# Cache pages laid four tokens to a partition: one page on 32 partitions

## The reference, cut to what matters

```python
z = x @ w_in                                   # q | k | v | B | C | h
page_sum = sum over tokens of cache_k[page]    # per page and head
gate  = q . (page_sum of the block's 2 pages) / 256
sel   = top 3 of the 8 past blocks by gate     # per sample and head
s     = q . k / 8 - slope[head] * (t - pos)    # over the tokens of the chosen blocks
out   = softmax(s) @ v
x1 = LayerNorm(alpha * x + concat(attn, conv) @ w_out)
y  = LayerNorm(alpha * x1 + (silu(a) * g) @ w_ffn_down)    # a, g = conv3(x1 @ w_ffn_up)
```

## Time and profile before

| | |
|---|---|
| median of 3 runs | 487.06 us |
| the profiled execution's own time | 488.61 us |
| its span in the profile | 486.8 us (1.8 us lie around it) |
| TensorE busy | 432.3 us, 89% |
| VectorE busy | 294.7 us, 61% |
| ScalarE busy | 184.4 us, 38% |
| read from device memory | 121.9 MB |
| SyncE's DMA queue | 107.55 MB |
| ScalarE's DMA queue | 16.78 MB |

### The profile page before, as it was taken

One profiled execution on the slowest core, in us unless ns is written; L12 is line 12 of the kernel. 1 busy time (PEld: TensorE's weight loads), 2 busy tenths in 40 slices (PEclk: granted clock), 3 DMA queues, 4 the chain that ended last, 5 costly groups with the idle time before them and its releaser, 6 DMA issues. The chain is left out here.

```text
span 486.8 us, 8294 instructions
## 1 busy us (share of the span) xinstructions
PE 432.3 (89%) x2951; PEld 352.1 (72%) x2951; DVE 294.7 (61%) x367; ACT 184.4 (38%) x713; POOL 84.1 (17%) x115
## 2 busy tenths in 40 slices
PE   5999969989899993799968797999999996999990
PEld 5678847866767761467524375999999996999990
DVE  0567769999989878526122245257777767243527
ACT  1566446764455433412001122245555553333300
POOL 1003000795120000000000240352122115000002
PEclk9999989999999998799979999899999998999996
DMA  8999998996959999999999963066666684576302
GB/s 306 339 326 386 396 387 312 340 337 196 398 188 374 386 395 355 335 339 340 356 363 357 367 186 88 1 174 174 174 174 179 183 223 119 153 205 170 87 1 89
DMA packets 115791, 124.85 MB, mean 256 GB/s; under 512 B 5866, under 2 KB 74291, under 8 KB 115704
## 3 DMA queue, kind: packets, MB, share of 16 engines
q1 hardware_dynamic: 108454, 107.55, 69.0%
q10 hardware_dynamic: 7296, 16.78, 9.6%
HBM read 121.90 MB, written 2.61 MB: 256 GB/s over the span
## 5 line engine op out<-in xcount | busy, mean ns | idle before, releaser
L1086 DVE TENSOR_TENSOR wlo<-KV,whi 128x2048 fp32r<-128x2048 f32 (+1 forms) x23 | 59.5, 2588 | 68.4 <-ACT whi L751 36.9
L1296 PE MATMUL ps<-xT,wring 128*128 128x264 f32 x384 | 92.5, 396 | 0.0
L837 DVE TENSOR_TENSOR qk<-KV,qk 128x2048 f32<-128x2048 f32 x32 | 74.0, 2315 | 26.9 <-DMA KV<-in_cache_k 17.1
L1296 PEld LDWEIGHTS ps<-xT,wring 128*128 128x128 f32 x384 | 73.2, 194 | 15.9 <-issue 4.0
L582 ACT ACTIVATE qk<-qk 128x64 f32<-128x64 f32 x224 | 53.8, 242 | 42.3 <-DVE qk L837 42.3
L1632 PE MATMUL ps<-x1h,whi 128*128 128x264 f32 x240 | 68.9, 287 | 0.4
L1634 PE MATMUL ps<-x1h,wlo 128*128 128x264 f32 x240 | 68.0, 283 | 0.0
L1633 PE MATMUL ps<-x1l,whi 128*128 128x264 f32 x240 | 68.0, 283 | 0.0
L845 DVE TENSOR_REDUCE T<-qk 128x24 f32<-128x1536 f32 (+1 forms) x32 | 58.0, 1812 | 0.0
L1632 PE MATMUL ps<-fh,whi 128*128 128x264 f32 x176 | 50.9, 289 | 4.7 <-POOL fl L545 4.7
L1633 PE MATMUL ps<-fl,whi 128*128 128x264 f32 x176 | 50.6, 288 | 0.0
(11 more groups left out here) (198 smaller groups left out, 596.6 us busy)
## 6 DMA issues: line engine op xcount, KB each, us to landing
KV<-in_cache_k SPq DMA_DIRECT2D x128, 256.0 KB, 6.6
KV<-in_cache_v SPq DMA_DIRECT2D x60, 256.0 KB, 4.8
KV<-in_w_ffn_up SPq DMA_DIRECT2D x30, 512.0 KB, 5.2
wring<-in_cache_v SPq DMA_DIRECT2D x56, 256.0 KB, 5.3
wring<-in_w_in ACTq DMA_DIRECT2D x6, 2048.0 KB, 14.4
KV<-in_w_ffn_down SPq DMA_DIRECT2D x8, 1408.0 KB, 7.0
zbuf<-in_cache_v SPq DMA_DIRECT2D x12, 256.0 KB, 6.2
zbuf<-in_w_ffn_up SPq DMA_DIRECT2D x6, 512.0 KB, 8.8
```

The lines of the kernel that those rows point to most:

```text
L837: nc.vector.tensor_tensor(prod[:, j % 2, :].rearrange("p (g d) -> p g d", g=GP), kv[:, s], q, ALU.mult).then_inc(s_kused, 1)
L1086: nc.vector.tensor_tensor(wlo[s][:, 0:n], w2[s][:, 0:n], whi[s][:, 0:n], ALU.subtract).then_inc(s_lo, 1)
L1296: ins = nc.tensor.matmul(ps[:, z_bank(n), 0:R], w[:, k, i * P:(i + 1) * P], xT[:, k, :], start=k == 0, stop=k == KT - 1)
```

## The change

Page `g` of a unit goes to partitions 32 g to 32 g + 31 instead of to all 128; each of those partitions gets four consecutive tokens, 8 KB in one run. The slot keeps its shape and its size; its second axis is now the token's place `j` among the four instead of the page. So partitions 0 to 63 of a unit hold its first gating block and partitions 64 to 127 its second. `gate_sums` multiplies with `headmask`, whose two columns are one on partitions 0 to 63 and 64 to 127, and sums the four `j`; `penalties` writes the block penalties to the two halves of the partitions with a matmul each; the table of distances is built for the new places. The multiplies, sums, exponentials, `values` and the order of the queues have the same text as before.

```diff
             def load(pages, ids, dst, landed):
                 for g in range(GP):
-                    sp.dma_start(dst[:, g, :], pages[bass.ds(ids[g], 1)].rearrange("o t d -> (o t) d")).then_inc(landed, 16)
+                    sp.dma_start(dst[32 * g:32 * g + 32], pages[bass.ds(ids[g], 1)].rearrange("o (p j) d -> (o p) j d", j=GP)).then_inc(landed, 16)
...
-                for k in range(NBLK):
-                    for t in range(2):
-                        ins = nc.tensor.matmul(ps[0:32, 5, k:k + 1], T[:, x, 2 * k + t, :], ones[:, 0:1],
-                                               start=t == 0, stop=t == 1)
+                for i in range(SLOTS):
+                    for j in range(GP):
+                        ins = nc.tensor.matmul(ps[0:32, 5, 2 * i:2 * i + 2], T[:, x, GP * i + j, :], headmask,
+                                               start=j == 0, stop=j == GP - 1)
...
-                blocks = penx.rearrange("q k (o m) -> q k o m", o=1).to_broadcast([32, NBLK, 2, 32])
-                nc.tensor.matmul(ps[:, 4, :], ones[0:32, :], blocks, start=False, stop=True).then_inc(s_penps, 1)
+                for i in range(2):
+                    blocks = penx.rearrange("q (s i) (o m) -> q i s o m", i=2, o=1)[:, i].to_broadcast([32, SLOTS, GP, 32])
+                    ins = nc.tensor.matmul(ps[64 * i:64 * i + 64, 4, :], ones[0:32, 0:64], blocks, start=False, stop=True)
+                ins.then_inc(s_penps, 1)
...
-    past = PAST - (np.arange(NPAGE)[None, :] * PAGE + tok[:, None])
+    col = np.arange(NPAGE)
+    past = PAST - (col[None, :] // GP * GP * PAGE + tok[:, None] * GP + col[None, :] % GP)
```

## The result

The changed kernel takes 628.87 us (median of 4 runs, 621.87 to 634.96) against 487.74 us (median of 4): a ratio of 1.285, 95% interval 1.273 to 1.297. The prediction was 634 us. The profiled execution took 627.06 us with a span of 625.3 us, 138.5 us more than before.

The account below looks back on a forecast made before the run. It took DMA transfers to bound the value stage, with VectorE, DMA and TensorE level in the key stage. 488.6 + 60 (key stage) + 87 (value stage) = 636, less 1.6 for the median: 634 us, range 548 to 668.

Parts of the forecast that it names:

- The rate: Cache page copies to 32 partitions: 210 GB/s instead of 387, taking a copy's rate to go with the partitions it writes.
- The value stage: From 141 to 284 us before: 38 units left, 39.8 MB, take 190 us at 210 GB/s instead of 103, +87 us.
- engines out of step: Rival, chance 0.20: engines drift onto different partitions, pages move at 272 GB/s, value stage +43 us, 567 us in all.
- The key stage: Keys and input projection, 8 to 141 us before: weights starved behind 8 KB rows, +60 us, bounds +8 and +75.
- The forecast's own list: Key stage followed tile by tile through TensorE's work: tiles 20 to 23 end at 209 us, 68 us late.
- The turn: Key stage, both queues active: 624 ns for 8 KB of keys plus 85 ns for 2 KB of `w_in`, 45 us a chunk.
- rival without starved weights: Rival, chance 0.18: rows cut into 2 KB packets, queues share evenly, key stage +33 us, 607 us in all.
- The compute side: Gate sums, penalties, multiplies, sums and values: taken as zero; penalty matmuls could cost up to 2.2 us.
- The last stage: The last 203 us, which don't touch the cache: carried over unchanged.
- TensorE's waits for value pages: Sign to look for after the change: these waits grow from about 20 to about 100 us.
- partitions don't matter: Rival, chance 0.12: longer rows bring 414 GB/s, value stage -7 us, key stage gives nothing, 480 us in all.

## Why the prediction was right, point by point

**The rate.** 210 GB/s forecast for pages alone, 217 measured. The number was right and the rule behind it wrong: it took the 103 to 110 GB/s on 16 partitions times two because the partitions double (which is 206 to 220, not the 230 that the sum has). 64 partitions together would by that rule have moved at the full rate, and they are at 218. What counts is whether a copy reaches one half of the 128 or both, and from 16 to 32 partitions the two readings happen to agree. That the estimate came out is in part luck; the same rule, asked about 64 partitions, would have missed by nearly half. Two figures that the prediction quotes can be held against the runs. The Trainium skill, "SBUF — State Buffer", section "Door 1: The DMA port swizzle", has two for partitions 0 to 31: the quoted 189 GB/s, for a transfer of 1 MiB, and about 218 as the limit. The trace agrees with the second: copies back to back moved 217. The section "Can I just issue two DMAs to hit both halves?" of the same page of the Trainium skill has a gain of 6%. Alternating the halves on one queue gained 11% here, 240 against 217 GB/s, and for this kernel the measurement decides.

**The value stage.** +87 forecast, +80 measured. The mechanism holds, but two errors in the sum cancel. Added up by size over the stage and spread over the 16 engines, the packets of the pages took 109 us before and 173 after: +64 and not +87. The measured 217 GB/s instead of 210 would have made it +81; the other 17 us are the faster stretches, 567 ns for an average packet of 8 KB in this stage against 607 from 12 to 20 us. If they are engines out of step, that rival was a part of the truth. On the other side the sum left the rest of the stage at 40 us, and it grew by some 15, of which 9 are one term: the packets of 512 B in which the early weights come took 46 us instead of 37, 40 ns each instead of 32.

**The key stage.** +60 forecast, +58 measured, but the steps came out otherwise than told, and errors on the way cancelled in part. Chunk 1 was to hold tile 4 back to 66 us; tile 4 came at 45.9. The key loads are queued behind the state rows and the constants, and these, not 8 KB rows, stood beside the weights at that time. DMA queues of the changed kernel from 34 to 44 us, and two copies of ScalarE's queue issued in that time (count, KB, us from issue to landing):

```profile
q10 hardware_dynamic: 789, 1.59, 54.9%
q1 hardware_dynamic: 901, 1.14, 49.6%
...
wring<-in_w_in ACTq DMA_DIRECT2D x1, 2048.0 KB, 40.9
wo_att<-in_w_out ACTq DMA_DIRECT2D x1, 2048.0 KB, 57.5
```

Tile 8 came at 80.6 (forecast 95), when chunk 2, issued at 39.6, landed after 40.9 us; the 18.09 us that its row puts down to "issue" end with this landing. Tile 12 came at 132.3 (135), after 28.7 us of waiting for chunk 3 behind `w_out`'s first half. So from tile 8 to tile 12 it took 52 us where the forecast had 40: it let the keys' queue run dry at 92 us because VectorE would wait for tile 7, and gave the weights the whole rate. In the trace VectorE waited for keys instead, and both queues went on side by side, here from 88 to 96 us:

```profile
q1 hardware_dynamic: 218, 1.18, 59.9%
q10 hardware_dynamic: 218, 0.88, 43.0%
```

The second value unit was issued at 199.4 (near 200). The forecast's own list ended at 209 and was taken 8 us lower by judgement, so that +60 came so close is in part luck.

The other error is the ratio of the bytes. From 100 to 130 us of the changed kernel, first the total:

```profile
DMA packets 1932, 7.27 MB, mean 242 GB/s; under 512 B 333, under 2 KB 333, under 8 KB 1284
...
q1 hardware_dynamic: 965, 5.29, 75.0%
q10 hardware_dynamic: 964, 1.95, 28.0%
```

The packets alternate, 965 to 964, as the prediction said; the bytes stand 2.7 to 1, not 4 to 1. 333 of the packets are under 512 B: for every two of 8 KB that a page gives an engine there is a small one that closes the copy, and it takes a turn of its own. So the weights got three turns for 16 KB of keys where the prediction gave them two. In these 30 us each of the 16 engines moved 60 packets of `w_in`, one in 0.50 us and not in 0.71, which makes 32 us for a chunk instead of 45; chunk 3 took 32 us, from `w_out`'s landing at 100.2 to its own at 132.2. The turn, at 709 ns, is the term that was mis-sized. The run with rows of 2 KB splits the 58 us: 26 went with the length of the packets and are the weights' waiting, 32 stayed and are the keys' own slower copies. The prediction's numbers had nearly this split, 27 and 33 (its rival without starved weights), though it says that the weights suffer more than the keys.

**The rest.** The compute side cost nothing (0.999). The last stage kept its 203 us. TensorE's waits for value pages were to grow from about 20 to about 100 us. Its matmuls' waits for them in the value stage came to 55 us, which is also what its idle time there grew by; the other 25 of the 80 us are longer instructions at the lower clock. The rival "partitions don't matter" is refuted, and "the weights are not starved" too, since 26 us of the key stage came back with short packets.

## What to carry to other kernels

Before a layout trades partitions for longer rows, ask whether one copy reaches both halves of the 128 partitions: 32 together or 64 together within a half moved at about half the rate, 32 or 64 spread evenly over all moved at the full one, and four neighbouring copies one after another didn't make up for each other. Where two queues share the engines, count packets, the small closing one among them: who sends long rows takes the time of who sends short ones. And a layout that is faster on the wire need not win. The two spread ones moved 6% more in the first copies and lost 9 and 14 us in all, probably because their copies take about as long to issue as to move.

## What the runs showed of the hardware that was not expected

- 64 partitions lying together are no faster than 32: 218 and 217 GB/s. Every second or fourth partition gives 410 and 411.
- How long SyncE takes to issue a copy of 256 KB depends on its shape: 316 ns for 32 whole rows together, 333 ns for 128 rows of 2 KB, 472 ns for every fourth partition, 475 ns for every second, 468 ns for 64 rows of 4 KB on neighbouring partitions. For 32 partitions in rows of 2 KB it took between 316 ns and a median of 629 ns for the keys.
- Where the partitions are spread, rows of 8 KB moved 6% more than rows of 2 KB (411 against 387 GB/s).
- Alternating the halves from page to page gives 240 instead of 217 GB/s.
- Two queues sent the same number of packets whatever the sizes: 965 to 964 with 8 KB against 2 KB. A load of `w_in` (2 MB) took up to 57.8 us to land, part of it behind `w_out`, and 17.7 at most before.
